# A two-layer hybrid decoder step on one core: the output projection's products issued in two row halves

## The reference, cut to what matters

```python
def merge_branches(p, o_a, o_b, o_c, w_up_a, w_up_b, w_up_c, w_out):
    gates = jax.nn.sigmoid(p['g_merge']).reshape(b, t, N_BRANCH, D_MODEL)
    m = (gates[:, :, 0] * ((o_a * jax.nn.silu(p['z_a'])) @ w_up_a)
         + gates[:, :, 1] * ((o_b * jax.nn.silu(p['z_b'])) @ w_up_b)
         + gates[:, :, 2] * ((o_c * jax.nn.silu(p['z_c'])) @ w_up_c))
    return (m @ w_out).astype(o_a.dtype)
...
    return x + y, (dil_states[0], dil_states[1], dil_states[2], win_state, conv_state, nsa_rows)
```

## Time and profile before

| | us |
|---|---|
| median of 3 runs | 944.43 (943.87 to 944.63) |
| the profiled execution | 943.71 |
| its span, first to last instruction | 942.0 |
| PE busy in the span | 922.4 (98%) |
| DVE busy | 652.9 (69%) |
| ACT busy | 462.2 (49%) |
| granted TensorE clock, mean | 0.998 |

### The profile page before, as it was taken

One profiled execution on the slowest core, in us unless ns is written; L12 is line 12 of the kernel. 1 busy time (PEld: TensorE's weight loads), 2 busy tenths in 40 slices (PEclk: granted clock), 3 DMA queues, 4 the chain that ended last, 5 costly groups with the idle time before them and its releaser, 6 DMA issues.

```text
span 942.0 us, 21760 instructions
## 1 busy us (share of the span) xinstructions
PE 922.4 (98%) x8064; PEld 858.3 (91%) x8064; DVE 652.9 (69%) x1481; ACT 462.2 (49%) x878; POOL 187.4 (20%) x321
## 2 busy tenths in 40 slices
PE   6999999999999999999999999999999999999997
PEld 6999988988888799999999999889888888999996
DVE  6999657667665567656769986666766565775574
ACT  6454746655544444334543556555645435443352
POOL 1200000226658500000000000003474672000000
PEclk9999999999999999999999999999999999999999
DMA  8762975536879974333666567647369799434421
GB/s 329 279 259 105 419 286 202 245 125 224 277 223 286 262 303 186 140 135 114 255 251 240 199 274 287 258 161 302 120 204 279 260 271 320 199 134 175 184 90 51
DMA packets 66345, 209.89 MB, mean 223 GB/s; under 512 B 12208, under 2 KB 49776, under 8 KB 56256
## 3 DMA queue, kind: packets, MB, share of 16 engines
q1 hardware_dynamic: 57200, 187.67, 54.2%
q0 software_dynamic: 8896, 20.81, 7.1%
q10 hardware_dynamic: 144, 0.01, 0.0%
HBM read 202.48 MB, written 41.36 MB: 259 GB/s over the span
## 4 chain that ended last, share of the span: by engine, by line
PE 89%; DVE 5%; issue 2%; ACT 2%; DMA 2%; SPq 0%; DVEq 0%; ACTq 0%
PE bank L1021 62%; PE bank L1241 9%; PE bank L1034 5%; PE bank L1161 3%; PE bank L1139 3%; PE bank L1275 1%; DMA big<-in_w_tok 1%; PE bank L1371 1%; PE bank L1174 1%; PE bank L1343 1%; DMA x<-in_x 1%; DVE short L1668 0%; DVE big_r L1728 0%; PE bank L1093 0%; PE bank L1220 0%
## 5 line engine op out<-in xcount | busy, mean ns | idle before, releaser
L1728 DVE TENSOR_TENSOR big_r<-big,paged_r 128x1024 fp32r<-128x1024 f32 (+1 forms) x160 | 194.9, 1221 | 80.8 <-ACT paged_r L1489 78.5
L1021 PE MATMUL bank<-xnT_high_r,paged_r 128*128 128x288 f32 x768 | 231.7, 302 | 0.0
L1021 PE MATMUL bank<-xnT_r,paged_r 128*128 128x288 f32 x704 | 207.6, 295 | 0.0
L1021 PE MATMUL bank<-xnT_high_r,big_r 128*128 128x288 f32 x704 | 207.0, 294 | 0.0
L1489 ACT ACTIVATE paged_r<-big 128x1024 fp32r<-128x1024 f32 (+1 forms) x160 | 166.6, 1048 | 5.6 <-DMA big<-in_w_feat 3.7
L1021 PE MATMUL bank<-short_r,big_r 128*128 128x288 f32 x568 | 167.5, 295 | 0.0
L1021 PEld LDWEIGHTS bank<-xnT_high_r,paged_r 128*128 128x128 f32 x768 | 144.0, 188 | 7.0 <-issue 5.3
L1021 PEld LDWEIGHTS bank<-xnT_high_r,big_r 128*128 128x128 f32 x704 | 132.5, 188 | 0.0
L1021 PE MATMUL bank<-short_r,paged_r 128*128 128x288 f32 x440 | 131.1, 298 | 1.2 <-DVE big_r L1728 1.0
L1021 PEld LDWEIGHTS bank<-xnT_r,paged_r 128*128 128x128 f32 x704 | 132.3, 188 | 0.0
L1021 PE MATMUL bank<-kvp_r,paged_r 128*128 128x288 f32 x440 | 130.3, 296 | 0.0
(11 more groups left out here) (340 smaller groups left out, 1842.6 us busy)
## 6 DMA issues: line engine op xcount, KB each, us to landing
big<-in_w_tok SPq DMA_DIRECT2D x13, 2048.0 KB, 9.0
big<-in_w_feat SPq DMA_DIRECT2D x12, 2048.0 KB, 8.3
big<-in_w_gate SPq DMA_DIRECT2D x10, 2048.0 KB, 9.1
out_kept_dil<-in_cache_dil SPq DMA_DIRECT2D x16, 1020.0 KB, 13.4
paged<-in_pool SPq DMA_DIRECT2D x218, 64.0 KB, 4.7
big<-in_w_up SPq DMA_DIRECT2D x12, 1024.0 KB, 8.8
paged<-in_pool POOLq DMA_DIRECT2D x166, 64.0 KB, 5.2
big<-in_kv_win SPq DMA_DIRECT2D x4, 2048.0 KB, 8.9
```

Source lines behind the costliest of these rows:

```text
L1021: last = mm(out, l, r, start=(c == 0 and i == 0), stop=(c == n - 1 and i == 2))
L1728: v.tensor_tensor(l_part[:, rest], full[:, rest], h_part[:, rest].bitcast(FP32), ALU.subtract)\
```

## The change

The three products per contraction tile become six: each is issued for the lower 64 partitions (into a bank of the ring O) and for the upper 64 (into the bank of PJ), in turn. The two banks are full at about the same time, and DVE adds first the one, then the other to x. PE additionally waits for the bank of O to be free, DVE for it to be full and, before the second addition, for the end of its own first one.

```diff
+        if k == "down":
+            o_keys.append((layer, ("o",) + s))
...
-                    precise(pj(s)[:, 0:T], lambda c: (wh[:, c, :], wl[:, c, :]),
-                            lambda c: (m_high[c], m_low[c]), KT, ("down", nh), q4,
-                            lambda c: merged.at((c // 4, 2, c % 4))).then_inc(*PJ.fill(s))
+                    okey = ("o",) + s
+                    wait(pe, O.is_free(okey))
+                    pe.wait_ge(*split_done.at(("split", ("down", nh), q4)))
+                    upper, lower = slice(0, HD), slice(HD, P)
+                    for c in range(KT):
+                        pe.wait_ge(*merged.at((c // 4, 2, c % 4)))
+                        for i, (w, m) in enumerate(((wh, m_high[c]), (wh, m_low[c]), (wl, m_high[c]))):
+                            ends = dict(start=(c == 0 and i == 0), stop=(c == KT - 1 and i == 2))
+                            of_lower = mm(ob(okey)[:, 0:T], w[lower, c, :], m[lower, :], **ends)
+                            of_upper = mm(pj(s)[:, 0:T], w[upper, c, :], m[upper, :], **ends)
+                            if ends["stop"]:
+                                of_lower.then_inc(*O.fill(okey))
+                                of_upper.then_inc(*PJ.fill(s))
...
+                    okey = ("o",) + s
+                    dve.wait_ge(*O.is_full(okey))
+                    v.scalar_tensor_tensor(part, ob(okey)[:, 0:T], 0.25, part, ALU.mult, ALU.add)\
+                        .then_inc(*O.release(okey))
+                    dve.wait_ge(*O.is_used(okey))
                     dve.wait_ge(*PJ.is_full(s))
                     v.scalar_tensor_tensor(part, pj(s)[:, 0:T], 0.25, part, ALU.mult, ALU.add).then_inc(*PJ.release(s))
```

## The result

The changed kernel took 947.14 us (median of 8 runs, 945.95 to 950.38), the kernel before 944.48 us (8 runs, 943.87 to 945.23): +2.66 us, a ratio of 1.0032 [1.0019, 1.0044]. An unchanged copy of it in a second series gave 947.28 against 944.83 us, +2.45 us, 1.0028 [1.0017, 1.0038]. It is slower, by a little more than the 0.2% that can be told here.

A forecast was written before the change was run, and what follows sets the result against it. It took PE's stream of matmuls, busy 922.4 of 942.0 us, as the bound. Layer 0's 1.55 us and layer 1's 1.2 gave 2.7, on 944.43 us 947.1; range 944.3 to 956.

The forecast's parts named there:

- part 1: "Down" steps on PE: a pair of halves takes 0.136 us against a full matmul's 0.133, 0.5 us per layer.
- part 2: PE, both ends of each layer's "down" steps: changing between halves and full rows costs 0.20 us each.
- The one out of halves in layer 0: PE behind layer 0's "down" steps: this 0.2 us change falls ahead of a wait, which swallows it.
- part 3: DVE's second addition: layer 0's cycle becomes 3.48 us, x 2.4 us late, next projection's products 1.4; 0.48 at the end.
- tile 2's shift: DVE in layer 0: tile 2 takes over 0.1 us of delay from the later first tiles.
- The tail: Program's end: the last tile's second addition between PE's end and ACT's square adds 0.48 us.
- Layer 1, 1.2 us: Layer 1's sum: PE's 0.2 us into halves, 0.5 for the pairs, and 0.48 for the last second addition.
- One after another: Rival on PE: the halves run serially, each pair 0.267 us, 51.2 us more, 996 us in all; chance 0.11.
- partly overlapped: Rival on PE: the halves overlap only in part, say 0.160 us a pair, 955.8 us in all; chance 0.11.
- Hidden loads: Rival on PE: halves hide the load's share of a matmul, 0.124 us a pair, 944.9 us; chance 0.12.
- Milder waits: Rival: the second addition's waits cost less because ACT or the sequencer lets tiles close up, 945.7 us; chance 0.12.
- PE waiting for a bank inside the steps: Sign against the forecast: PE held by a bank inside the "down" steps, where it expected none.

The follow-up runs named there:

- after: The changed kernel itself, in halves with two additions, against the kernel before: 947.14 against 944.48 us, ratio 1.0032.
- halves_one_add: Changed kernel, but the lower half goes to a bank nothing reads and DVE adds once: 945.32 us against 944.83 for the kernel before, 1.0003.
- apart: Changed kernel with all 24 products of one half ahead of the 24 of the other: 984.10 us against 944.76 for the kernel before, 1.0414.
- add_twice: Kernel before, full-row matmuls, but DVE adds the same bank twice at half weight: 947.32 against 944.83 us, 1.0025.
- after_split_first: Changed kernel with the split of the next weights moved ahead of the low part of x: 946.58 us against 944.83 for the kernel before, 1.0018.

## Why the prediction was right, and where it was off

I forecast 947.1 us and 947.14 came, by the mechanism I named. Part of that closeness is luck: my terms sum to 2.7, the lags of the same places to 2.30, while the medians' +2.66 and +2.45, each with about 1 us of doubt, can't tell the two apart.

- **A pair at 0.136 us, 0.5 us a layer** (part 1): mis-sized. It measured 0.133, so the term is zero, in after as in halves_one_add. The mistake was to carry 3 ns over from two columns of rounded times in the short score blocks, smaller than what those rows resolve. That fp32r pairs run side by side, the step with the wide bounds, held: 0.133, far from 0.267 and 0.160, and apart shows what they would cost without it.
- **0.20 us for a mode change** (part 2), read off one place in the scores: right at every place, 0.19 to 0.20 in both directions, and 0.19 in a kernel with fourteen of them inside the steps. The Trainium skill's "TensorEngine Tiling (Array Packing)", section "Key Properties", says that a change of tiling mode drains the engine; the trace agrees, and gives the price. Where my part 2 speaks of a mode change at every half, it is the change of tile that is meant; it costs nothing, at 0.133 us a pair.
- **The one out of halves in layer 0 lies beneath the wait** (part 2): right. It shows as 0.19 in the table's second row, but without it the wait would be that much longer, since c = 7 starts when DVE has x. The layer's total is 1.61 us, forecast 1.55. With the pairs' 0.5 us gone, the wait took the place of it too, which is why mis-sizing them cost the layer nothing.
- **DVE's cycle of 3.48 us, x 2.4 us late, PE waiting about 1 us** (part 3): right, with 3.49, 2.36 and 0.94. But the "about 1 us" of idle did not follow from my sum: products 1.4 us late, 0.9 of it PE's own delay, leave 0.5. It came to 0.94 because the pairs' 0.5 fell away. My 0.1 us for tile 2's shift held as well (10.19 against 10.12 us after the first product), yet in add_twice, where the load of w_out came later, the same shift was 0.47: the agreement of layer 0's total to 0.06 us is in part luck. add_twice has the wait without halves, halves_one_add halves without the wait, after_split_first both halves and additions without it. That leaves only the cycle's length as its cause.
- **The tail, 0.48 us**: 0.49 in every kernel whose two banks are full together, nothing with one addition, and 0.07 in apart, where the first bank is full half a step earlier and its addition is done by then.
- **Layer 1, 1.2 us**: 0.20 + 0.49 = 0.69, the same 0.5 of the pairs. Its tiles did not fall behind PE's products so as to show.
- **Rivals.** One after another (996) and partly overlapped (955.8) fall with 0.133 us a pair. Hidden loads (944.9) falls too: a half alone paces like a full matmul and a pair no better. That rival rested, on the page's side, on the Trainium skill's "TensorE: Matmul & The Clock Gate", section "The mechanism", that a load overlaps matmuls only where its rows differ (the section also names a background weight buffer as a way to load ahead of matmuls in flight, which I had passed over); the runs show no gain from loads on other rows. Milder waits (945.7) falls with 1.61 and 0.49, and add_twice shows that such a wait can as well be harsher.
- **PE waiting for a bank inside the steps**, which would have proved me wrong: not in after, nor in any other kernel. In add_twice PE is 0.10 us late right behind the steps, at the next projection's first product (472.89): DVE's second addition of tile 6, which frees that bank, ends at 472.83. In after the same addition ends 0.7 us before PE comes.

Open: nothing here tells why halves 24 apart overlap for three matmuls and no more, why SP's issues were slow in some executions, nor why the load of w_out landed later in add_twice (8.5 us from its issue against 7.9 in after).

## What to carry to other kernels

Splitting a product by rows gives two matmuls that run side by side at the price of one, so on PE it gains nothing and costs 0.2 us at each change of mode; the price is paid where the two halves are summed. Before adding an operation to an engine that is "69% busy", look at its cycle in the stage where it works tile after tile with a dependent chain: 3.00 us against 3.20 was slack of 0.2, and an addition of 0.48 made DVE the slower. If such an operation must be added, first fill the waits inside the cycle: moving an independent 1.2 us operation into one took the whole wait back.

## What the runs showed of the hardware that I had not expected

- Side-by-side running isn't bound to neighbours: halves three apart overlap fully (a step of 3.20 us) and start out of the list's order, halves 24 apart for some three matmuls at each meeting (5.53 us instead of 6.40).
- A half-row matmul alone takes the full one's 0.133 us from start to start, although its load has half the rows.
- After PE's idle of 2.44 us the granted clock averaged 0.72 over the 6 us around it, and a block of 16 matmuls took 3.61 us, not 1.90: one late page cost 4.1 us in that execution.
- Most of SP's issues take 0.33 us, but each trace has 14 to 19 of 447 that take over 1 us. In after four of them (1.07 to 1.84 us) fell among the 17 issues of one group of loads.
